# Routing in groups of one head instead of two, with scores made for two queries at a time

## The chip, the core and the metric

The kernel runs on one core of a Trainium2 chip. The metric is the device time of one execution in microseconds. Five engines work side by side, each on its own list of instructions in order, and wait for each other through semaphores: PE (TensorE, matrix products), ACT (ScalarE), DVE (VectorE), POOL (GpSimd) and SP (SyncE, which only issues transfers here).

## The reference, cut to what matters

One layer of an encoder: 512 frames and 16 meta tokens of 1,024 features, a token mixer, then the product-key expert layer (`peer`) that this change is about:

```python
q = jnp.einsum('nd,dhk->nhk', x, w_q)                      # 8 heads, 256 wide
q1, q2 = jnp.split(q, 2, axis=-1)
s1 = jnp.einsum('nhk,hmk->nhm', q1, sub_keys[:, 0])        # 128 keys each
s2 = jnp.einsum('nhk,hmk->nhm', q2, sub_keys[:, 1])
v1, i1 = lax.top_k(s1, PEER_TOPK)                          # PEER_TOPK = 16
v2, i2 = lax.top_k(s2, PEER_TOPK)
cand = (v1[..., :, None] + v2[..., None, :]).reshape(N, PEER_HEADS, 256)
sc, sel = lax.top_k(cand, PEER_TOPK)                       # 16 experts of 16,384
gate = jax.nn.softmax(sc, axis=-1)
a = jnp.einsum('nd,ned->ne', xk, u_emb[ek])                # then gelu(a) * gate
out = jnp.einsum('ne,ned->nd', coef, v_emb[ek])
```

The kernel computes the activations of all 16,384 experts for all frames as 128 "up tiles" and picks with the gates afterwards; so an up tile doesn't need the routing.

## The kernel before, in words

Float32 products are made in three passes: each operand is split into a high half (an ACT copy that rounds, L1438) and a low half (the difference, L1443, by POOL or DVE), and `three_pass` (L368) issues three matmuls for each of 8 slices, 24 in all, for one tile of 128 x 512. Both kinds of tile of this stage are made so: a **query** (`wq`; 16 of them, two for each head, the weights in rings of three) and an **up tile** (`ut`; 24 of the 128 are made in this stage, the others after it).

The stage is `route` (L1483). It begins and ends with a barrier of all engines. Frames are taken in NB = 4 blocks of 128. Queries are taken in groups of G = 4 (two heads); a group gives four **steps** n, one for each block, 16 in all. A step is:

- PE `scores(n)`: a matmul with each of the G queries (L1593) into one bank of PSUM. In its list PE has scores(n+1), then the queries of step n, then the up tiles of step n.
- ACT `copy_scores(n)` to SBUF (L1634). ACT also copies finished queries (`copy_q`, L1628), makes the high half of the query three further on right behind it (`split_q`), and finishes up tiles (gelu, L1474, and the high half of the tile two further on).
- DVE `top16` (L1679) on G key lists of 128: max, match_replace, max, then the indices. `settle` waits after each of the first three groups of instructions for its last one. Then `rank_candidates(n - 1)` does the same on G/2 candidate lists of 256.
- POOL: the low halves of the queries that are three ahead (`low_q`), then the candidate sums of step n (L1822), which wait for DVE's key ranking of step n, then the low halves of the up tiles of step n + 1. All in this order in one list.
- SP: loads of weights, stores of up tiles, and the zeroing of the gate map in 32 stores, dealt over the steps.

Which query and which up tile stands in which step is set by two small tables (L1539, L1540). Behind the steps PE has twelve more up tiles (`sel_up` to 23), beside which DVE turns the ranked places into expert numbers (`hits`, `take`, `sums`, `addresses`) and makes the low halves of these tiles. Behind the stage's barrier, `experts` (L1857) scatters the gates with 384 indirect transfers of POOL, finishes the 104 other up tiles and makes the down products.

The stage before, `mix_rows`, makes queries 0 and 1 at its end. `route` begins with queries 2 and 3, in banks of their own, before the first scores.

Of the kernel before, what the change touches and what calls it, by code (L numbers as in the profile page):

```python
# [23 lines left out]
P = 128  # L24
# [4 lines left out]
NB = FRAMES // P  # L29
# [44 lines left out]
SLOTS = PEER_HEADS * PEER_TOPK  # L74
ZERO_ROWS = 4
WQ_RING = 3
ZERO_STORES = P // ZERO_ROWS


# [1403 lines left out]
def route(c, x_hi, x_lo, places, expert, gates, zeroed, wq, ut, nc, io, sem, sb, psum, ident, iota, gates_d, acts_d, acts_s, **_):  # L1483
# [4 lines left out]

    G = 4
    SETS = 2 * PEER_HEADS
    NG = SETS // G
    STEPS = NG * NB
    K = PEER_TOPK
    sub_keys = sb("sub_keys", [P, SETS, NKEYS], c=c)
    q_t = sb("q_t", [P, 2 * G, FRAMES], c=c)
# [1 line left out]
    work = sb("key_work", [P, G, NKEYS], c=c)  # L1499
    top_v = sb("top_v", [P, NB, SETS, K], c=c)  # L1500
    top_i = sb("top_i", [P, NB, SETS, K], U32, c=c)
    cand = sb("cand", [P, 2, 2, K * K], c=c)
    cand_work = sb("cand_work", [P, 2, K * K], c=c)
    best = sb("best", [P, NB, PEER_HEADS, K], c=c)
    place = sb("place", [P, NB, PEER_HEADS, K], U32, c=c)
    place_half = sb("place_half", [P, 2, PEER_HEADS, K], U32, c=c)
# [29 lines left out]
    sel_up = ROUTE_TILES - SEL * NB  # L1536
    queries, ups, j, t = [], [], G, 0
    for n in range(STEPS):
        q = min(SETS - j, (1, 1, 2, 0)[n % NB])  # L1539
        m = min(sel_up - t, (0, 0, 1, 1)[n % NB] if n + G < SETS else (2, 1, 2, 1)[n % NB])  # L1540
        queries.append(list(range(j, j + q)))
        ups.append(list(range(t, t + m)))
        j, t = j + q, t + m
    assert j == SETS and t == sel_up and STEPS == SETS

    with nc.Block() as block:
        @block.sync
        def _(sp):
            def load_q(j):
                wq.load(sp, io["peer_wq"], j)  # L1550

            def next_up(t):
                ut.load(sp, io["peer_u"], t + ut.RAW)
                ut.store(sp, acts_d, acts_s, t)

            def store_zeros(x):
                rows = slice(x * ZERO_ROWS, (x + 1) * ZERO_ROWS)
                sp.dma_start(gates_d[:, rows], zeros[:].unsqueeze(1).broadcast_to([P, ZERO_ROWS, DENSE])).then_inc(zeroed, 16)

            sp.dma_start(sub_keys[:], io["sub_keys"]).then_inc(keys_in, 16)  # L1560
            sp.wait_ge(zeros_done, 1)
            for t in range(2, ut.RAW):
                ut.load(sp, io["peer_u"], t)
            for j in range(G, G + WQ_RING):
                load_q(j)
            for n in range(STEPS):
                for j in queries[n]:
                    if j + WQ_RING < SETS:
                        load_q(j + WQ_RING)
                for t in ups[n]:  # L1570
                    next_up(t)
                for x in range(n * ZERO_STORES // STEPS, (n + 1) * ZERO_STORES // STEPS):
                    store_zeros(x)
            for t in range(sel_up, ROUTE_TILES):
                next_up(t)

        @block.tensor
        def _(pe):
            def query_bank(j):

                return psum[:, (2 + j if j < G else j % 2), :]

            def query(j):
                wq.product(nc, pe, x_hi, x_lo, j, j % WQ_RING, j < G, query_bank(j))

            def scores(n):
                g, b = divmod(n, NB)
# [10 lines left out]
            def up(t):  # L1598
                ut.product(nc, pe, x_hi, x_lo, t, t % 2, t < 2)

            for j in range(2, G):
                query(j)
            pe.wait_ge(keys_in, 16)
            for n in range(STEPS):
                if n == 0:
# [12 lines left out]
        def _(act):  # L1618
# [3 lines left out]
            def copy_q(j):  # L1622
                g, x = divmod(j, G)
                act.wait_ge(wq.product_done, j + 1)
                if g >= 2:
                    act.wait_ge(s_done, (g - 1) * NB)
                bank = wq.bank[j % 2] if j < 2 or j >= G else psum[:, 2 + j, :]
                nc.scalar.activation(q_t[:, g % 2 * G + x], bank, ACT.Copy).then_inc(wq.bank_read, 1)  # L1628

            def copy_scores(n):  # L1630
                act.wait_ge(s_done, n + 1)
                if n >= 2:
                    act.wait_ge(s_read, n - 1)
                nc.scalar.activation(s[:, n % 2].rearrange("p g m -> p (g m)"), psum[:, 2 + n % 4, :],  # L1634
                                     ACT.Copy).then_inc(s_copied, 1)

            def split_u(t):
# [6 lines left out]

            for j in range(G):
                copy_q(j)
                if j + WQ_RING >= G:
                    split_q(j + WQ_RING)
            for n in range(STEPS):
                if n == 0:  # L1650
                    copy_scores(n)
                if n and n - 1 + G < SETS:
                    for t in ups[n - 1]:
                        finish_up(t)
                if n + 1 < STEPS:
# [5 lines left out]
                if n + G >= SETS:  # L1661
                    for t in ups[n]:
                        finish_up(t)
            act.wait_ge(centered, NB)
# [7 lines left out]
        def _(dve):  # L1672
# [24 lines left out]
            def rank_candidates(n):  # L1697
                g, b = divmod(n, NB)
                dve.wait_ge(cand_done, n + 1)
                top16(2, lambda x: cand[:, n % 2, x], lambda x: cand_work[:, x], lambda x: best[:, b, 2 * g + x],  # L1700
                      lambda x: place[:, b, 2 * g + x], cand_read)

            def low_u(t):
                ut.split_lo(nc.vector, dve, t)
# [98 lines left out]
        def _(pool):  # L1803
# [6 lines left out]
            for j in range(G, G + WQ_RING):  # L1810
                low_q(j)
            for n in range(STEPS):
                g, b = divmod(n, NB)
# [3 lines left out]
                pool.wait_ge(s_read, n + 1)  # L1817
                if n >= 2:
                    pool.wait_ge(cand_read, n - 1)
                for x in range(2):  # L1820
                    head = 2 * g + x
                    last = nc.gpsimd.tensor_tensor(  # L1822
                        cand[:, n % 2, x].rearrange("p (i j) -> p i j", j=K),
                        top_v[:, b, 2 * head].unsqueeze(2).broadcast_to([P, K, K]),
# [383 lines left out]
```

## Time and profile before

| what | us |
|---|---|
| three timed runs | 2107.15, 2117.3, 2119.26 (median 2117.3) |
| the profiled execution: its own time | 2101.18 |
| its span, first to last instruction | 2099.3 |
| in it: up to the routing stage | 422.5 |
| the routing stage | 422.5 to 656.6 |
| gates scattered, up tiles go on | 656.6 to about 1240 |
| remaining up tiles and all down products | to 2099.3 |

The stages were read from the timelines: the first instructions of `route` start at 422.5 (L1558 to L1628), the first up tile of `experts` after the barrier at 657.0. A busy engine is one that has an instruction running; PE's matmuls overlap, so its busy time tells little, and its waits tell more. In a timeline the number in brackets is the time for which the engine sat idle before the instruction, with the instruction or transfer that released it.

### The profile page before, as it was taken

To read this page: it belongs to the slowest core of one execution; us is meant where nothing else is said; L and a number is where in the kernel's file an instruction comes from. 1 tells how busy PE (TensorE), PEld (TensorE's weight loads), DVE (VectorE), ACT (ScalarE), POOL (GpSimd) and SP (SyncE) were. 2 spreads that over 40 slices of the span, in tenths; PEclk is the share of its full clock that TensorE was granted. 3 is DMA by queue.
4 is the path that set the end of the run, shared out by engine and by line. 5 is a ranking of instruction groups with operands and counts; after the bars stand their busy time and mean duration, and the time that the engine had idled before them with its cause. 6 is when DMAs were issued, how large, how long until landed. Compare 5 with 4: busy or idle time off the path is not lost.

```text
span 2099.3 us, 23531 instructions
## 1 busy us (share of the span) xinstructions
PE 1764.5 (84%) x7878; PEld 1430.3 (68%) x7878; DVE 1130.1 (54%) x2971; ACT 576.7 (27%) x924; POOL 909.3 (43%) x800
## 2 busy tenths in 40 slices
PE   5999999999999444663724499999999999999998
PEld 4867778888877233441613278888888888888886
DVE  3269784569986212330503222222236888888886
ACT  4332152332232000110201022222233333333333
POOL 4643200053502667667675640000007767777730
PEclk9999999999999667775856699999999999999999
DMA  4322220258754111220302146444449999999992
GB/s 134 97 61 66 46 70 33 81 197 290 246 196 131 46 38 53 75 76 15 106 16 60 46 127 226 150 141 144 148 141 386 391 376 365 368 374 364 378 357 76
DMA packets 182675, 351.05 MB, mean 167 GB/s; under 512 B 35600, under 2 KB 118928, under 8 KB 182448
## 3 DMA queue, kind: packets, MB, share of 16 engines
q1 hardware_dynamic: 147776, 282.74, 40.4%
q0 software_dynamic: 34816, 67.41, 9.0%
q8 instruction: 27, 0.44, 0.1%
q14 instruction: 56, 0.46, 0.1%
HBM read 289.04 MB, written 61.02 MB: 167 GB/s over the span
## 4 chain that ended last, share of the span: by engine, by line
PE 47%; another core or an unknown queue 14%; issue 5%; ACT 2%; DVE 1%; ACTq 0%; DVEq 0%
PE psum L370 16%; PE psum L372 16%; PE psum L371 16%; ACT ts_hi_u L1438 1%; DVE ts_lo_u L1443 0%; ACT sparse_rows L2068 0%; DVE mixed L1995 0%; DVE mixed L1983 0%; DVE v_lo L1934 0%; ACT v_hi L2051 0%; ACTq L1473 0%; ACT rstd_final L2071 0%; DVE rstd_final L795 0%; DVE rstd_final L799 0%
## 5 line engine op out<-in xcount | busy, mean ns | idle before, releaser
L370 PE MATMUL psum<-x_hi,ts_hi_u 128*128 128x512 f32 x1024 | 419.9, 410 | 188.5 <-issue 108.3
L1443 DVE TENSOR_TENSOR ts_lo_u<-ts_raw_u,ts_hi_u 128x1024 fp32r<-128x1024 f32 x116 | 142.1, 1225 | 681.3 <-ACT ts_hi_u L1438 577.6
L2146 POOL DMA_INDIRECT gate_map<-gate_total,gate_at x384 | 388.5, 1012 | 264.1 <-DVE same_expert L1917 159.8
L372 PE MATMUL psum<-x_hi,ts_lo_u 128*128 128x512 f32 x1024 | 416.3, 407 | 51.6 <-issue 51.5
L371 PE MATMUL psum<-x_lo,ts_hi_u 128*128 128x512 f32 x1024 | 415.2, 406 | 45.6 <-issue 45.5
L370 PEld LDWEIGHTS psum<-x_hi,ts_hi_u 128*128 128x128 f32 x1024 | 202.5, 198 | 250.4 <-issue 148.9
L2134 POOL DMA_INDIRECT sparse_rows<-in_peer_v,v_row x128 | 160.1, 1251 | 425.3 <-PE psum L372 330.9
L1474 ACT ACTIVATE ut_out_u<-psum 128x512 f32<-128x512 f32 x128 | 76.5, 597 | 837.2 <-PE psum L372 395.5
L370 PE MATMUL psum<-v_hi,c_hi 128*128 128x512 f32 x768 | 298.8, 389 | 0.0
L371 PE MATMUL psum<-v_lo,c_hi 128*128 128x512 f32 x768 | 298.8, 389 | 0.0
L372 PE MATMUL psum<-v_hi,c_lo 128*128 128x512 f32 x768 | 298.8, 389 | 0.0
L372 PEld LDWEIGHTS psum<-x_hi,ts_lo_u 128*128 128x128 f32 x1024 | 201.7, 197 | 101.2 <-issue 59.2
L371 PEld LDWEIGHTS psum<-x_lo,ts_hi_u 128*128 128x128 f32 x1024 | 202.5, 198 | 93.1 <-issue 52.9
L2051 ACT ACTIVATE v_hi<-v_raw 128x1024 fp32r<-128x1024 f32 x128 | 135.8, 1061 | 310.0 <-PE psum L372 265.1
L1934 DVE TENSOR_TENSOR v_lo<-v_raw,v_hi 128x1024 fp32r<-128x1024 f32 x128 | 157.0, 1226 | 79.8 <-ACT v_hi L2051 63.4
L2140 POOL DMA_INDIRECT sparse_act<-up_acts_sparse,act_at x128 | 171.8, 1342 | 40.3 <-issue 38.7
L370 PEld LDWEIGHTS psum<-v_hi,c_hi 128*128 128x128 f32 x768 | 144.2, 188 | 30.0
L371 PEld LDWEIGHTS psum<-v_lo,c_hi 128*128 128x128 f32 x768 | 144.2, 188 | 29.8
L372 PEld LDWEIGHTS psum<-v_hi,c_lo 128*128 128x128 f32 x768 | 144.2, 188 | 29.8
L1438 ACT ACTIVATE ts_hi_u<-ts_raw_u 128x1024 fp32r<-128x1024 f32 x128 | 134.5, 1052 | 0.0
L370 PE MATMUL psum<-whi_in,h_hi 128*128 128x512 f32 (+1 forms) x280 | 110.2, 394 | 2.4 <-PEq L268 2.4
L1917 DVE SCALAR_TENSOR_TENSOR same_expert<-expert,gates 128x128 f32<-128x128 f32 x384 | 108.2, 347 | 1.4 <-DVE same_expert L1917 1.4
(235 smaller groups left out, 2345.6 us busy)
## 6 DMA issues: line engine op xcount, KB each, us to landing
ts_raw_u<-in_peer_u SPq DMA_DIRECT2D x128, 512.0 KB
v_raw<-in_peer_v SPq DMA_DIRECT2D x128, 512.0 KB
gate_map<-zeros SPq DMA_DIRECT2D x32, 768.0 KB, 5.9
up_acts<-ut_out_u SPq DMA_DIRECT2D x128, 192.0 KB
act_in<-up_acts SPq DMA_DIRECT2D x128, 192.0 KB
gate_in<-gate_map SPq DMA_DIRECT2D x128, 192.0 KB
raw_in<-in_w_in SPq DMA_DIRECT2D x56, 256.0 KB, 2.8
ts_raw_wq<-in_peer_wq SPq DMA_DIRECT2D x16, 512.0 KB, 7.4
```

Source lines behind the costliest of these rows:

```text
L370: nc.tensor.matmul(out, l_hi, r_hi, start=first, stop=False)
L371: nc.tensor.matmul(out, l_hi, r_lo, start=False, stop=False)
L372: return nc.tensor.matmul(out, l_lo, r_hi, start=False, stop=last)
L1438: nc.scalar.activation(self.hi[:, n % self.slots], self.raw[:, n % self.raws], ACT.Copy).then_inc(self.hi_done, 1)
L1443: eng_ops.tensor_tensor(self.lo[:, n % self.slots], self.raw[:, n % self.raws], self.hi[:, n % self.slots].bitcast(F32), ALU.subtract).the ...
L1474: nc.scalar.activation(self.out[:, i], self.bank[n % 2], ACT.Gelu).then_inc(self.bank_read, 1)
L1917: nc.vector.scalar_tensor_tensor(out=dn.same[:, j % 2], in0=expert[:, b], scalar=expert[:, b, j:j + 1], in1=gates[:, b].rearrange("p h k - ...
L1934: nc.vector.tensor_tensor(dn.v_lo[:, i], dn.v_raw[:, e % RAW], dn.v_hi[:, i].bitcast(F32), ALU.subtract).then_inc(v_lo_done, 1)
L2051: nc.scalar.activation(dn.v_hi[:, i], dn.v_raw[:, e % RAW], ACT.Copy).then_inc(v_hi_done, 1)
L2134: nc.gpsimd.indirect_dma_start(dn.rows[:, r], None, v_rows, bass.IndirectOffsetOnAxis(places["v_row"][:, j:j + 1], 0)).then_inc(row_in[r], 16)
L2140: nc.gpsimd.indirect_dma_start(dn.picked[:, j:j + 1], None, act_cells, bass.IndirectOffsetOnAxis(places["act_at"][:, j:j + 1], 0)).then_in ...
L2146: nc.gpsimd.indirect_dma_start(gate_cells, bass.IndirectOffsetOnAxis(places["gate_at"][:, b, j:j + 1], 0), dn.total[:, b, j:j + 1], None). ...
```

## The change

G becomes 2, one head. A group still has four steps, one for each block, so there are 32 steps in place of 16, each with half the work: two score matmuls in place of four, copied as 128 x 256; two key lists ranked, one candidate list made and ranked. Scores begin once queries 0 and 1 are there; queries 2 and 3 move behind the first scores, and share the two banks of the others. The two tables get new patterns: in a group, steps 0 and 1 have a query each, step 2 an up tile, step 3 nothing; in the last four steps (`n >= ASKING`) there are 2, 1, 1, 1 up tiles. Seven up tiles stand in the first 28 steps and five in the last four, in place of six in the first 12 and six in the last four. Number and size of the tiles, of the transfers and of the ranked lists are the same.

```diff
+EARLY_Q = 4
...
-    G = 4
+    G = 2
+    HEADS = G // 2
     NG = SETS // G
     STEPS = NG * NB
+    ASKING = STEPS - NB
...
     for n in range(STEPS):
-        q = min(SETS - j, (1, 1, 2, 0)[n % NB])
-        m = min(sel_up - t, (0, 0, 1, 1)[n % NB] if n + G < SETS else (2, 1, 2, 1)[n % NB])
+        q = min(SETS - j, (1, 1, 0, 0)[n % NB])
+        m = min(sel_up - t, (0, 0, 1, 0)[n % NB] if n < ASKING else (2, 1, 1, 1)[n % NB])
...
-            for j in range(G, G + WQ_RING):
+            for j in range(EARLY_Q, G + WQ_RING):
                 load_q(j)
...
-            for j in range(2, G):
-                query(j)
             pe.wait_ge(keys_in, 16)
...
-                nc.scalar.activation(s[:, n % 2]..., psum[:, 2 + n % 4, :],
+                nc.scalar.activation(s[:, n % 2]..., psum[:, 2 + n % 4, 0:G * NKEYS],
...
-                if j + WQ_RING >= G:
+                if j + WQ_RING >= EARLY_Q:
                     split_q(j + WQ_RING)
...
-                if n and n - 1 + G < SETS:
+                if n and n - 1 < ASKING:
                     for t in ups[n - 1]:
                         finish_up(t)
...
-                top16(2, lambda x: cand[:, n % 2, x], ...
+                top16(HEADS, lambda x: cand[:, n % 2, x], ...
...
-                for x in range(2):
-                    head = 2 * g + x
+                for x in range(HEADS):
+                    head = HEADS * g + x
```

Two places of the lists show what moves. First POOL, around the low half of the up tile with number 2 (`ts_lo_u`; `ts_lo_wq` is the low half of a query, `cand` the candidate sums). Before, from step 5:

```order
L1443 TENSOR_TENSOR ts_lo_wq<-ts_raw_wq,ts_hi_wq 128x1024
L1822 TENSOR_TENSOR cand<-top_v 128x256 x2
L1443 TENSOR_TENSOR ts_lo_u<-ts_raw_u,ts_hi_u 128x1024
L1443 TENSOR_TENSOR ts_lo_wq<-ts_raw_wq,ts_hi_wq 128x1024 x2
L1822 TENSOR_TENSOR cand<-top_v 128x256 x2
```

And now, from step 8:

```order
L1444 TENSOR_TENSOR ts_lo_wq<-ts_raw_wq,ts_hi_wq 128x1024
L1822 TENSOR_TENSOR cand<-top_v 128x256
L1444 TENSOR_TENSOR ts_lo_wq<-ts_raw_wq,ts_hi_wq 128x1024
L1822 TENSOR_TENSOR cand<-top_v 128x256
L1444 TENSOR_TENSOR ts_lo_u<-ts_raw_u,ts_hi_u 128x1024
L1822 TENSOR_TENSOR cand<-top_v 128x256 x2
```

The low half of the up tile stands in both behind a query's low half and the candidate sums. Before, two more queries follow behind it for the same step, and PE has these two queries ahead of the up tile; now no query of the step follows.

Second ACT at the start of the stage (`q_t` are copied queries, `ts_hi_wq` high halves of query weights, `key_scores` copied scores). Before:

```order
L1628 ACTIVATE q_t<-psum 128x512 x2
L1438 ACTIVATE ts_hi_wq<-ts_raw_wq 128x1024
L1628 ACTIVATE q_t<-psum 128x512
L1438 ACTIVATE ts_hi_wq<-ts_raw_wq 128x1024
L1628 ACTIVATE q_t<-psum 128x512
L1438 ACTIVATE ts_hi_wq<-ts_raw_wq 128x1024
L1634 ACTIVATE key_scores<-psum 128x512 x2
```

And now:

```order
L1628 ACTIVATE q_t<-psum 128x512 x2
L1439 ACTIVATE ts_hi_wq<-ts_raw_wq 128x1024
L1634 ACTIVATE key_scores<-psum 128x256 x2
L1628 ACTIVATE q_t<-psum 128x512
L1439 ACTIVATE ts_hi_wq<-ts_raw_wq 128x1024
L1634 ACTIVATE key_scores<-psum 128x256
```

The first scores are copied two queries earlier, but still behind one high half, that of query 4.

## Rows read from the trace of the kernel before

**Rows 1.** Windows by stage: busy us of each engine, PE clock, DMA share, GB/s.

```profile
422.50:656.60 234.10, 224.25 (x1040) 186.91 (x1040) 198.03 (x853) 71.14 (x99) 76.24 (x57) 0.99 0.65 224
656.60:1240.00 583.40, 305.43 (x1057) 225.91 (x1057) 158.60 (x812) 67.45 (x88) 388.51 (x384) 0.70 0.21 59
```

**Rows 2.** Timeline of ACT, routing: start, us, instruction, idle before and releaser.

```profile
566.99 0.60 ACT L1474 ACTIVATE ut_out_u<-psum 128x512 f32<-128x512 f32 x1 [4.32 <-PE psum L372]
...
573.34 0.60 ACT L1474 ACTIVATE ut_out_u<-psum 128x512 f32<-128x512 f32 x1 [4.31 <-PE psum L372]
...
578.78 0.60 ACT L1474 ACTIVATE ut_out_u<-psum 128x512 f32<-128x512 f32 x1 [3.89 <-PE psum L372]
...
654.79 0.60 ACT L1474 ACTIVATE ut_out_u<-psum 128x512 f32<-128x512 f32 x1 [3.89 <-PE psum L372]
```

**Rows 3.** Waits of PE in the routing stage: us, times, longest.

```profile
PE psum L370 <- DVE ts_lo_u L1443: 4.7, 2, 3.2
...
PE psum L1593 <- ACT q_t L1628: 2.0, 1, 2.0
PE psum L370 <- POOL ts_lo_u L1443: 1.3, 1, 1.3
```

**Rows 4.** Timeline of DVE, the first ranking of four lists.

```profile
438.30 0.87 DVE L1683 MAX8 top_v<-key_scores 128x8 f32<-128x128 f32 x4 [14.68 <-ACT key_scores L1634]
439.21 0.09 DVE L1686 MATCH_VALUE_LOAD key_work<-top_v,key_scores 128x8 f32 x1
...
443.41 0.85 DVE L1683 MAX8 top_v<-key_scores 128x8 f32<-128x128 f32 x4
```

**Rows 5.** Timeline of DVE, the first ranking of two candidate lists.

```profile
450.06 0.76 DVE L1683 MAX8 best<-cand 128x8 f32<-128x256 f32 x2 [1.49 <-POOL cand L1822]
...
454.15 0.85 DVE L1683 MAX8 top_v<-key_scores 128x8 f32<-128x128 f32 x4
```

**Rows 6.** One line's instructions: count, ns min/median/max.

```profile
L1683 DVE MAX8 top_v<-key_scores x64: 271/276/295, 438.3 to 577.6; 128x8 f32<-128x128 f32 x64
```

**Rows 7.** Timeline of DVE at the end of the ranking.

```profile
587.29 0.75 DVE L1683 MAX8 best<-cand 128x8 f32<-128x256 f32 x2
...
591.38 1.20 DVE L1443 TENSOR_TENSOR ts_lo_u<-ts_raw_u,ts_hi_u 128x1024 fp32r<-128x1024 f32 x1
```

**Rows 8.** The key table's load, from issue to landing.

```profile
DMA to landing us min/median/max: 4.9/4.9/4.9
```

**Rows 9.** Timeline of ACT at the routing stage's start.

```profile
432.55 1.06 ACT L1438 ACTIVATE ts_hi_wq<-ts_raw_wq 128x1024 fp32r<-128x1024 f32 x1 [8.91 <-DMA ts_raw_wq<-in_peer_wq]
...
437.68 0.60 ACT L1634 ACTIVATE key_scores<-psum 128x512 f32<-128x512 f32 x1 [1.21 <-PE psum L1593]
```

**Rows 10.** Timeline of ACT, a query copied, the next one's high half.

```profile
487.46 0.60 ACT L1628 ACTIVATE q_t<-psum 128x512 f32<-128x512 f32 x1 [0.78 <-PE psum L372]
490.67 1.06 ACT L1438 ACTIVATE ts_hi_wq<-ts_raw_wq 128x1024 fp32r<-128x1024 f32 x1 [2.62 <-DMA ts_raw_wq<-in_peer_wq]
```

**Rows 11.** Timeline of POOL behind that high half.

```profile
491.81 2.41 POOL L1443 TENSOR_TENSOR ts_lo_wq<-ts_raw_wq,ts_hi_wq 128x1024 fp32r<-128x1024 f32 x1 [2.00 <-ACT ts_hi_wq L1438]
494.18 1.20 POOL L1822 TENSOR_TENSOR cand<-top_v 128x256 f32<-128x256 f32 x2
495.34 2.42 POOL L1443 TENSOR_TENSOR ts_lo_u<-ts_raw_u,ts_hi_u 128x1024 fp32r<-128x1024 f32 x1
```

**Rows 12.** Timeline of PE, a tile after a pause (weight loads left out).

```profile
690.63 0.79 PE L370 MATMUL psum<-x_hi,ts_hi_u 128*128 128x512 f32 x1 [4.51 <-DVE ts_lo_u L1443]
...
694.63 0.63 PE L370 MATMUL psum<-x_hi,ts_hi_u 128*128 128x512 f32 x1
...
695.58 0.40 PE L370 MATMUL psum<-x_hi,ts_hi_u 128*128 128x512 f32 x1
```

**Rows 13.** Windows after a pause of PE: columns as Rows 1.

```profile
436.00:438.00 2.00, 2.00 (x11) 2.00 (x11) 0.00 (x0) 0.79 (x2) 2.00 (x2) 0.50 0.55 33
588.00:590.00 2.00, 2.00 (x10) 1.67 (x9) 1.90 (x9) 0.00 (x0) 0.00 (x0) 1.00 1.06 397
```

More of the change, by code:

```diff
@@ L1501, in route @@
     top_i = sb("top_i", [P, NB, SETS, K], U32, c=c)
-    cand = sb("cand", [P, 2, 2, K * K], c=c)
-    cand_work = sb("cand_work", [P, 2, K * K], c=c)
+    cand = sb("cand", [P, 2, HEADS, K * K], c=c)
+    cand_work = sb("cand_work", [P, HEADS, K * K], c=c)
     best = sb("best", [P, NB, PEER_HEADS, K], c=c)
@@ L1543, in route @@
         j, t = j + q, t + m
-    assert j == SETS and t == sel_up and STEPS == SETS
+    assert j == SETS and t == sel_up
     with nc.Block() as block:
@@ L1579, in query_bank @@
             def query_bank(j):
-                return psum[:, (2 + j if j < G else j % 2), :]
+                return wq.bank[j % 2]
             def query(j):
-                wq.product(nc, pe, x_hi, x_lo, j, j % WQ_RING, j < G, query_bank(j))
+                wq.product(nc, pe, x_hi, x_lo, j, j % WQ_RING, j < 2, query_bank(j))
             def scores(n):
@@ L1626, in copy_q @@
                     act.wait_ge(s_done, (g - 1) * NB)
-                bank = wq.bank[j % 2] if j < 2 or j >= G else psum[:, 2 + j, :]
-                nc.scalar.activation(q_t[:, g % 2 * G + x], bank, ACT.Copy).then_inc(wq.bank_read, 1)
+                nc.scalar.activation(q_t[:, g % 2 * G + x], wq.bank[j % 2], ACT.Copy).then_inc(wq.bank_read, 1)
             def copy_scores(n):
@@ L1633, in copy_scores @@
                     act.wait_ge(s_read, n - 1)
-                nc.scalar.activation(s[:, n % 2].rearrange("p g m -> p (g m)"), psum[:, 2 + n % 4, :],
+                nc.scalar.activation(s[:, n % 2].rearrange("p g m -> p (g m)"), psum[:, 2 + n % 4, 0:G * NKEYS],
                                      ACT.Copy).then_inc(s_copied, 1)
@@ L1660, in _ @@
                         split_q(j + WQ_RING)
-                if n + G >= SETS:
+                if n >= ASKING:
                     for t in ups[n]:
@@ L1699, in rank_candidates @@
                 dve.wait_ge(cand_done, n + 1)
-                top16(2, lambda x: cand[:, n % 2, x], lambda x: cand_work[:, x], lambda x: best[:, b, 2 * g + x],
-                      lambda x: place[:, b, 2 * g + x], cand_read)
+                top16(HEADS, lambda x: cand[:, n % 2, x], lambda x: cand_work[:, x], lambda x: best[:, b, HEADS * g + x],
+                      lambda x: place[:, b, HEADS * g + x], cand_read)
             def low_u(t):
@@ L1809, in _ @@
                 ut.split_lo(nc.gpsimd, pool, t)
-            for j in range(G, G + WQ_RING):
+            for j in range(EARLY_Q, G + WQ_RING):
                 low_q(j)
```

## The prediction

> **What bounds the kernel now.** I read four views, in this order. The windows by stage come first [rows 1]: the change lies in the stage from 422.5 to 656.6 us. In it PE has matmuls running for 224 of 234 us at a granted clock of 0.99, DVE is busy for 198, and ACT and POOL for about 75 each, so only PE or DVE can set this stage's end. In the next stage PE is busy for 305 of 583 us and POOL for 389. That stage begins behind a barrier of all engines and depends on nothing that the change touches but its start, so every us by which routing ends later is, to first order, a us of the whole.
>
> Then ACT's timeline, because ACT takes up each finished tile and so marks PE's pace [rows 2]. Two tiles with nothing between are 578.78 - 573.34 = 5.44 us apart. A tile with one score step ahead of it takes 573.34 - 566.99 = 6.35, so a score step of four queries costs PE 0.91. The last tile is done at 654.8, and the barrier follows at 656.6: PE ends the stage.
>
> Then PE's waits [rows 3]: 4.7 + 2.0 + 1.3 = 8.0 us. PE's work is 38 tiles x 5.44 = 206.7, and 16 score steps x 0.91 = 14.6. With the waits that is 229.3 of the 232.3 between 422.5 and 654.8. PE has next to nothing to give, and it depends on the order of the others' lists.
>
> Last DVE's timeline. Ranking four lists takes 443.41 - 438.30 = 5.11 us [rows 4], ranking two candidate lists 454.15 - 450.06 = 4.09 [rows 5]. Sixteen of both make 147 us of the 153 between 438.3, where ranking begins, and 591.4, where it ends [rows 4, 7]. So PE and DVE are nearly balanced through the steps.
>
> **The change part by part.**
>
> *Split ranking, DVE.* The same 64 + 32 lists are ranked, but the three waits of each ranking come twice as often. One MAX8 lasts 0.276 us [rows 6], four in a row 0.87 [rows 4], so starts are (0.87 - 0.276) / 3 = 0.20 apart and 0.08 of each is covered by the next. Behind a wait that cover is lost, and 439.21 - (438.30 + 0.87) = 0.04 comes on top [rows 4]. That is 0.12 for a wait; six new ones for each old step make 0.72, over 16 steps 11.5 us. A new step takes (5.11 + 4.09 + 0.72) / 2 = 4.96 us, and 32 of them 159 us. The Trainium skill weighs against this sum: "VectorE: DVE Perf Modes", section "The DRAIN you can't avoid", says that a semaphore behind every operation costs nothing over one behind the last. By it the 11.5 would be 0. The rows show the overlap that a wait takes away, and I go by them; no wait of the forecast's sum hangs on it.
>
> *Start.* Scores no longer stand behind queries 2 and 3, but behind the key table. It lands 4.9 us after its issue [rows 8], at 427.4, so PE waits 4.9 where it waited 2.0 [rows 3]: +3 on PE. DVE gains less than the 10.9 us of two tiles: ACT's copy of the first scores still has the high half of query 4 ahead, whose weights land at 432.5 [rows 9]. Ranking starts at about 433.7 in place of 438.3.
>
> *The up tile behind its low half.* This is the term that decides. In steps 8 to 11, 12 to 15 and 16 to 19 the order on PE is: scores, query, scores, query, scores, up tile. This tile's low half is POOL's, and in POOL's list it stands behind the low half that follows the second of these queries. That low half waits for ACT's high half, which reuses the query's slot and so waits for PE to finish this very query. The trace has the same chain once at full length: the query's copy starts at 487.46, the high half at 490.67 behind its load [rows 10], then POOL makes a low half, the sums of two heads, and the up tile's low half until 497.76 [rows 11]. That is 10.3 us. Before, it lay beside two further queries, 10.9 us of PE's work, and PE waited 1.3 [rows 3]. Now there is one score step of 0.45 beside it. The chain itself is shorter by one head's sums, 0.6. With the load's wait as in the row it is 9.7, without any (2.7 less) 7.0; I take 8.4, the middle, since the load is issued at the same point of the cycle but behind one zeroing store less. So PE waits 8.4 - 0.5 = 7.9, and a group takes 3 x 5.44 + 4 x 0.45 + 7.9 = 26.0 us where DVE's work is 4 x 4.96 = 19.9. Three groups: 23.7 - 1.3 = +22.4; the ends are 6.5 and 9.2 for each, or +18 and +26.
>
> *The later groups.* In steps 20 to 23 only the first query still has a successor, so a part of the chain lies beside the second query: 8.4 less 5.9 of query and scores would leave 2.5, but the candidate sums of step 21 wait for DVE, which is a step late by then; I take 5, between 2.5 and 7.9. In steps 24 to 31 there are six up tiles whose low halves stand behind sums paced by DVE's 4.96 us for a step: I take 2 + 3.5, between 0 and 10 in all. Sum +10.5.
>
> *The end.* The waits before tiles 12 and 14, 4.7 us [rows 3], came about because PE was ready before DVE had ranked. PE is now the later one, so they go: -4.7, or 0 at worst.
>
> *The clock.* Behind a pause of 4.5 us [rows 12] matmuls start (694.63 - 690.63) / 9 = 0.44 us apart, where a tile at full rate has 5.44 / 24 = 0.23; from 695.58 they are fast again. So the first 4 to 5 us after such a pause run at the lower level, 1.2 in place of 2.4 GHz, and cost 10 x 0.21 = 2 us. A pause of 2.0 did so too (at 436), one of 3.2 did not (at 588) [rows 3, 13]. Four pauses of 5 to 8 us make +8, between 0 (DVE could hide them) and +14. The start had a slow stretch before and has one now: 0.
>
> *At nothing.* ACT's 16 added copies are halves of the old ones; ACT is idle for two thirds of the stage [rows 1]. POOL's sums are as many as before. On SP every load and store keeps its place against its tile; zeroing goes from two stores a step to one, and must be done only before the scatters. If that cover went, a store in front of a load would lengthen the chain above, which its upper end holds.
>
> **Sum:** 3 + 22.4 + 10.5 - 4.7 + 8 = +39. DVE's catching up inside the blocked groups overlaps a little of the clock's term; I take off 2. Routing ends at 654.8 + 37 = 692 and the profiled execution goes from 2101.2 to 2138. That execution is faster than all three timed runs. The middle of the four times (2101.2, 2107.2, 2117.3, 2119.3) is 2112; the forecast for a median is 2112 + 37 = **2149 us**.
>
> **Rivals.**
>
> *DVE's pace (not slower).* If the up tiles' low halves come in time, PE waits 5 at the start and then runs through 26 tiles and all scores until 427.4 + 141.4 + 14.6 = 583.4, while DVE ranks until 433.7 + 158.7 = 592.4 instead of 591.4. The tail behind the ranking is as before, so routing ends 1 us later: 2113. For it: the balance is good on paper, 18.1 us of PE's work to 19.9 of DVE's in a group. Against it: the chain is forced by three lists in order. It decides if PE's waits for `ts_lo_u` stay below 2 us a group. By the page of the Trainium skill named above, the 11.5 us of waits would be nothing as well, PE would end the stage 6 us earlier (583.4 + 12 x 5.44 = 648.7), and the time would be about 2106.
>
> *The clock stays low.* If after each of the four pauses a whole tile and more runs at the lower level, each costs 5.4 in place of 2.0: +14, or 2163. For it: in the next stage, where PE is busy for half of the time, the mean clock is 0.70 [rows 1]. Against it: there the pauses are far longer.
>
> *The next stage gives it back, or more.* Its POOL work is 384 scatters, and PE's tiles wait for loads there. A shift of its start could shuffle these by some 10 us in either direction (the runs' own spread is 12). A gain of over 1% would need 60 us of it.
>
> **Chances.** The chain as forecast: 0.78. DVE's pace: 0.13. The clock stays low: 0.07. A gain out of the next stage: 0.02. About 1%, 21 us, is what a measurement of this kernel tells from no change. The chain at its lowest (3 + 18 + 2.5 - 4.7 + 0 = +19) lies just below it. So slower by over 1%: 0.82; within 1%: 0.16; faster: 0.02. The range takes in the chain's lower bound on the fastest timed run (2107 + 19) and the low clock on the slowest (2119 + 37 + 14): about 2127 to 2172.
>
> **What would show it.** PE's waits in the stage: `ts_lo_u` of POOL, five to seven times, 30 us or more in total, the longest 7 to 9; PE waits 5 us for the key table; the tiles after the pauses at half rate, the stage's clock near 0.9; first key ranking at 433 to 435; last candidate ranking at 615 to 625; a step of DVE without waits 4.96. The barrier comes at 685 to 700. I am wrong if PE's waits for `ts_lo_u` stay below 10 us, or if the next stages don't keep their 1443 us within 15.

## The result and the profile after

The changed kernel takes a median of 2139.6 us over four runs (2127.02 to 2142.17) beside 2116.37 for the kernel before (2107.15 to 2119.26), a ratio of 1.0148 with a 95% interval of 1.009 to 1.0205. Ratios in this document are made from the runs within 1.5% of the fastest of the same kernel and are not the quotients of the two medians, which is 1.011 here (23.2 us). Its profiled execution took 2138.91 us with a span of 2137.1, against 2101.18 and 2099.3. Routing's last up tile is done at 689.03 instead of 654.79: +34.2 us. The span is longer by 37.8.

The windows by stage of the changed kernel, columns as in [rows 1]:

```profile
422.50:600.00 177.50, 143.21 (x645) 119.11 (x646) 138.08 (x696) 42.01 (x73) 66.50 (x50) 0.90 0.58 206
600.00:700.00 100.00, 97.77 (x436) 80.78 (x435) 72.60 (x161) 31.85 (x44) 9.01 (x6) 1.00 0.54 170
700.00:1270.00 570.00, 287.82 (x984) 211.83 (x983) 154.61 (x809) 62.95 (x82) 387.55 (x384) 0.70 0.20 58
```

The loss is all in the first window: PE is idle for 34 of 177.5 us and its granted clock is 0.90. What PE waited for between 418 and 700 us (total, times, longest), to be laid beside [rows 3]:

```profile
PE psum L371 <- POOL ts_lo_u L1444: 29.8, 5, 7.3
PE psum L1596 <- DMA sub_keys<-in_sub_keys: 5.6, 1, 5.6
```

The waits of before for DVE's `ts_lo_u` (4.7) and for `q_t` (2.0) are gone, as is POOL's 1.3. The timeline of PE has each pause in brackets, with what ended it:

```profile
426.90 2.08 PE L1596 MATMUL psum<-sub_keys,q_t 128*128 128x128 f32 x8 [5.61 <-DMA sub_keys<-in_sub_keys]
...
484.68 0.79 PE L371 MATMUL psum<-x_hi,ts_hi_u 128*128 128x512 f32 x1 [7.06 <-POOL ts_lo_u L1444]
...
511.99 0.80 PE L371 MATMUL psum<-x_hi,ts_hi_u 128*128 128x512 f32 x1 [7.33 <-POOL ts_lo_u L1444]
...
538.98 0.80 PE L371 MATMUL psum<-x_hi,ts_hi_u 128*128 128x512 f32 x1 [7.00 <-POOL ts_lo_u L1444]
...
564.23 0.80 PE L371 MATMUL psum<-x_hi,ts_hi_u 128*128 128x512 f32 x1 [5.11 <-POOL ts_lo_u L1444]
...
595.30 0.50 PE L371 MATMUL psum<-x_hi,ts_hi_u 128*128 128x512 f32 x1 [3.27 <-POOL ts_lo_u L1444]
```

The first three pauses come 27 us apart, once in each group of four steps, the fourth 25 us later and the last behind the queries. One of them, followed back on ACT and then on POOL:

```profile
498.36 0.60 ACT L1628 ACTIVATE q_t<-psum 128x512 f32<-128x512 f32 x1 [4.25 <-PE psum L373]
502.36 1.06 ACT L1439 ACTIVATE ts_hi_wq<-ts_raw_wq 128x1024 fp32r<-128x1024 f32 x1 [3.40 <-DMA ts_raw_wq<-in_peer_wq]
503.32 0.36 ACT L1634 ACTIVATE key_scores<-psum 128x256 f32<-128x256 f32 x1
504.26 0.60 ACT L1628 ACTIVATE q_t<-psum 128x512 f32<-128x512 f32 x1 [0.57 <-PE psum L373]
505.58 1.06 ACT L1439 ACTIVATE ts_hi_wq<-ts_raw_wq 128x1024 fp32r<-128x1024 f32 x1 [0.72 <-DMA ts_raw_wq<-in_peer_wq]
```

```profile
503.49 2.36 POOL L1444 TENSOR_TENSOR ts_lo_wq<-ts_raw_wq,ts_hi_wq 128x1024 fp32r<-128x1024 f32 x1 [12.39 <-ACT ts_hi_wq L1439]
505.81 0.62 POOL L1822 TENSOR_TENSOR cand<-top_v 128x256 f32<-128x256 f32 x1
506.71 2.34 POOL L1444 TENSOR_TENSOR ts_lo_wq<-ts_raw_wq,ts_hi_wq 128x1024 fp32r<-128x1024 f32 x1 [0.28 <-ACT ts_hi_wq L1439]
509.01 0.62 POOL L1822 TENSOR_TENSOR cand<-top_v 128x256 f32<-128x256 f32 x1
509.59 2.35 POOL L1444 TENSOR_TENSOR ts_lo_u<-ts_raw_u,ts_hi_u 128x1024 fp32r<-128x1024 f32 x1
```

From the second query's copy (504.26) to the end of the up tile's low half (511.94) it is 7.7 us, and the tile starts at 511.99. This is the chain of [rows 10, 11] (10.3 us there), with nothing but a score step of PE's beside it. POOL had been idle for 12.39 us just before: it is late by its order, not by its load.

DVE without waits, the candidate rankings of three steps in a row:

```profile
587.19 0.41 DVE L1683 MAX8 best<-cand 128x8 f32<-128x256 f32 x1
...
592.15 0.41 DVE L1683 MAX8 best<-cand 128x8 f32<-128x256 f32 x1
...
597.12 0.41 DVE L1683 MAX8 best<-cand 128x8 f32<-128x256 f32 x1
```

A step is 4.97 us. Ranking begins at 432.50, and DVE goes on to the gates at 626.47, where before did so at 592.50.

### The profile page after: what moved, and what is told of

It reads as the page before. It is cut to its first block, busy times and chain, and to the rows that moved or that the text cites. A ratio compares the mean times of both kernels' runs of the same rounds, so it can differ in the third digit from the quotient of the medians.

```text
span 2137.1 us, 23589 instructions
## 1 busy us (share of the span) xinstructions
PE 1771.1 (83%) x7878; PEld 1434.6 (67%) x7878; DVE 1140.7 (53%) x2971; ACT 578.1 (27%) x940; POOL 914.0 (43%) x800
## 4 chain that ended last, share of the span: by engine, by line
PE 44%; another core or an unknown queue 16%; issue 3%; ACT 2%; DVE 2%; ACTq 0%; DVEq 0%
PE psum L373 15%; PE psum L371 15%; PE psum L372 15%; ACT ts_hi_u L1439 1%; DVE ts_lo_u L1444 1%; DVE same_expert L1917 0%; ACT sparse_rows L2068 0%; DVE mixed L1995 0%; DVE mixed L1983 0%; DVE v_lo L1934 0%; ACT ut_out_u L1475 0%; ACT v_hi L2051 0%; ACTq L1474 0%; ACT rstd_final L2071 0%
## 5 line engine op out<-in xcount | busy, mean ns | idle before, releaser
L2140 POOL DMA_INDIRECT sparse_act<-up_acts_sparse,act_at x128 | 174.0, 1359 | 40.1 <-issue 40.1
L373 PEld LDWEIGHTS psum<-v_hi,c_lo 128*128 128x128 f32 x768 | 144.1, 188 | 29.9
L372 PEld LDWEIGHTS psum<-v_lo,c_hi 128*128 128x128 f32 x768 | 144.1, 188 | 29.9
```

The lines of the kernel that those rows point to most:

```text
L372: nc.tensor.matmul(out, l_hi, r_lo, start=False, stop=False)
L373: return nc.tensor.matmul(out, l_lo, r_hi, start=False, stop=last)
L2140: nc.gpsimd.indirect_dma_start(dn.picked[:, j:j + 1], None, act_cells, bass.IndirectOffsetOnAxis(places["act_at"][:, j:j + 1], 0)).then_in ...
```

## The experiments

The sets of runs fell on different chips. In three sets the kernel before takes 2105 to 2123 us, in the fourth 1758.75 (see the last section). Routing lies ahead of the stage in which they differ, so its traces compare across chips; medians are compared only with those of the same set. The place from which routing starts differs between traces by up to 2.8 us: PE's first scores start at 426.90 in the first trace of the changed kernel and at 429.65 in the last. Some of the expectations call the kernel with the low half a whole group earlier e6, and the one with the first scores first as well e7.

### The changed kernel again

> The changed kernel once more, beside the others of this call. Theory (the up tile's low half behind the query's chain in POOL's list): routing's last tile at 687 to 692 us in the profile, PE waits for ts_lo_u 28 to 32 us in all, and the time 1.1 to 1.8% over the kernel before. Rival (later stages give part of the shift back): the same profile of the routing stage, but a ratio below 1.011.

Beside before at 2123.37 us it took 2157.96, ratio 1.018 (1.014 to 1.0221). Waits for POOL's `ts_lo_u`: 28.1 us in 6, longest 6.9; last routing tile 689.35. All this is as the theory had it. A third time, in a later set:

> The changed kernel once more, beside e6 and the combined kernel, for a reading of all of them against one set of runs of before. Theory A (the +34 us of the last routing tile are passed on one to one, whatever the clock of the stages behind is): the median is 32 to 36 us above before's; if before runs at about 1759 us again, where no stage behind had a granted clock of 0.7, that is a ratio of 1.018 to 1.021, against 1.015 and 1.018 where before took 2116 and 2123 us. Theory B (the stages behind stretch or absorb part of the shift by their clock): a difference outside 28 to 40 us.

It took 2145.22 us beside 2105.14, ratio 1.0244 (1.0176 to 1.0311), with waits of 29.4 in 5 and the last tile at 694.07, 2.8 of it from the later start. The difference of medians, 40.1 us, lies just beyond what theory A and even 28 to 40 allowed, but the 17 runs of before in that set spread from 2080.64 to 2117.59, so it doesn't tell the theories apart. The three intervals have 1.0176 to 1.0205 in common.

### The low half one step earlier

```diff
             for n in range(STEPS):
...
+                if n + 1 < ASKING:
+                    for t in ups[n + 1]:
+                        if t >= 2:
+                            ut.split_lo(nc.gpsimd, pool, t)
                 for j in queries[n]:
...
-                for t in ups[n + 1] if n + 1 < STEPS else []:
+                for t in ups[n + 1] if ASKING <= n + 1 < STEPS else []:
```

> The changed kernel, with one thing moved on POOL: the low half of the next step's up tile comes ahead of the query's low half and the candidate sums, in all steps but the last four. Theory: PE's four waits of 5 to 7 us before tiles 2 to 5 go below 1 us each and with them the slow clock behind them; routing's last tile falls from 689 to 656 to 662, since DVE's 32 steps of 4.96 us then set the pace, and the time comes within 0.4% of the kernel before. Rival A (DVE's split ranking is the real limit, and PE's waits only mirror it): the waits change places but the last tile stays above 675. Rival B (loads or ACT): PE's waits move to ts_hi or to the queries, last tile 665 to 680.

It took 2145.15 us, ratio 1.0121 (1.008 to 1.0163): better than the changed kernel of the same set by 12.8 us, but the waits only shrank from 28.1 to 19.6 us in 5. The last tile came at 679.67, 9.7 earlier, of which 0.8 is an earlier start (PE's first scores at 427.11 and 427.96). The size that the theory gave was wrong, and the last tile is above the 675 of rival A, though the waits didn't change places. POOL's timeline says why:

```profile
500.39 2.37 POOL L1444 TENSOR_TENSOR ts_lo_wq<-ts_raw_wq,ts_hi_wq 128x1024 fp32r<-128x1024 f32 x1 [8.20 <-ACT ts_hi_wq L1439]
502.71 0.62 POOL L1826 TENSOR_TENSOR cand<-top_v 128x256 f32<-128x256 f32 x1
503.29 2.34 POOL L1444 TENSOR_TENSOR ts_lo_u<-ts_raw_u,ts_hi_u 128x1024 fp32r<-128x1024 f32 x1
```

The up tile's low half had only passed the second of the group's two query low halves. The first was still ahead of it, and with it ACT's high half, for which POOL waited 8.20 us. So this run doesn't decide on rival A; the next one does.

### The low half a whole group earlier

The edit is shown against the kernel just above:

```diff
-                if n + 1 < ASKING:
-                    for t in ups[n + 1]:
+                if n % NB == NB - 1 and n + 3 < ASKING:
+                    for t in ups[n + 3]:
```

> The changed kernel, with POOL making the low half of an up tile a whole group of four steps earlier (just ahead of the candidates of the step before a group begins), so that it stands behind none of the low halves of query weights that came ahead of it. In the kernel with the low half only a step earlier TensorE still waited 3.9 to 4.3 us four times, because ACT's high half of the query weight and its DMA wait stood between. Theory A (the order on POOL's queue is the whole cost): TensorE's waits for this low half are under 1 us in groups 2 to 6, four falls of the clock go too, and the last routing tile ends at 656 to 664 us (before 654.8, changed kernel 689.0 and 689.4); ratio 1.000 to 1.006. Theory B (the ranking on DVE with its 96 more waits, or the query weights' loads, is a second bound close below): the waits for the low half vanish but others for q_t or ts_lo_wq take their place, last tile 665 to 678, ratio 1.007 to 1.012.

On the chip where before takes 1758.75 us it took 1774.1, ratio 1.0086 (1.0072 to 1.01). The ratio and the last tile (671.09) lie in the ranges of theory B, but not for its reason: the five pauses are gone, and no other wait took their place in the groups; there is one new wait, once, at the first tile behind the queries. PE's timeline, and POOL's with the low half that ends it:

```profile
558.15 1.13 PE L1596 MATMUL psum<-sub_keys,q_t 128*128 128x128 f32 x8 [0.76 <-ACT q_t L1628]
574.99 0.80 PE L371 MATMUL psum<-x_hi,ts_hi_u 128*128 128x512 f32 x1 [15.71 <-POOL ts_lo_u L1444]
```

```profile
572.02 0.62 POOL L1826 TENSOR_TENSOR cand<-top_v 128x256 f32<-128x256 f32 x1 [4.35 <-DVE top_i L1694]
572.60 4.68 POOL L1444 TENSOR_TENSOR ts_lo_u<-ts_raw_u,ts_hi_u 128x1024 fp32r<-128x1024 f32 x2
```

PE has run ahead until it has nothing left: the next tile's low half stands behind the candidate sums of step 27, which DVE paces. DVE now goes on to the gates at 608.54, and the last tile is 17.9 us earlier than in the changed kernel and 16.3 later than before. The run again, beside the changed kernel on one of the slower chips:

> The kernel with the low half a whole group earlier once more, beside the changed kernel. It took 15.4 us more than before (1774.1 against 1758.75), its last routing tile ended 16.3 us later. Theory A: it lies 17 to 20 us under the changed kernel here, which is what the order on POOL's queue and the falls of the clock behind it cost. Theory B: less than 12 us under it; then much of the difference to the earlier readings came from the chip and not from the order.

2123.71 us against 2145.22, 21.5 us less, with the same 15.7-us wait; the last tile came at 669.48, and from PE's first scores on that is 22.9 us less than in the changed kernel (241.49 and 264.42). Theory A had the cause, and its 17 to 20 us are a little too few. Beside before the ratio is 1.0153 (1.0099 to 1.0207).

### And the first scores first

```diff
             for j in range(G):
                 copy_q(j)
-                if j + WQ_RING >= EARLY_Q:
-                    split_q(j + WQ_RING)
...
                 if n + 1 < STEPS:
                     copy_scores(n + 1)
+                if n == 0:
+                    split_q(EARLY_Q)
```

> The kernel with the low half a whole group earlier, and ACT copies the first scores ahead of the high half of the fifth query weight, in place of behind it (that copy stood behind a DMA wait of 8.1 us and ended at 432.5 in the changed kernel). Theory A (DVE's ranking is what is late once TensorE's pauses are gone): the first ranking starts at 428 to 429, the whole routing moves with it by 3 to 4 us, last tile 653 to 660, ratio 0.998 to 1.004. Theory B (TensorE's own work sets the pace then): ranking starts earlier, but the last tile stays within 1 us of the kernel without this edit.

1773.92 us, ratio 1.0085 (1.0071 to 1.0098), the same as without this edit. Ranking starts at 429.02, 4.0 us earlier, and then waits for the first candidates, whose sums stand on POOL behind the low half of another query:

```profile
440.76 0.43 DVE L1683 MAX8 best<-cand 128x8 f32<-128x256 f32 x1 [6.17 <-POOL cand L1826]
```

Where the kernel without it waited 2.82 there. So 3.35 of the 4.0 are given back, and the last tile comes at 669.97, 1.1 earlier. Theory A had the start right and the gain wrong; theory B had the gain nearly (within 1 us), but not for its reason: PE still waits 15.71 us for the same low half.

### And both remaining waits

```diff
-        m = min(sel_up - t, (0, 0, 1, 0)[n % NB] if n < ASKING else (2, 1, 1, 1)[n % NB])
+        m = min(sel_up - t, (0, 0, 1 + (n == ASKING - 2), 0)[n % NB] if n < ASKING else 1)
...
-                for j in queries[n]:
+                for j in queries[n] if n >= 2 else []:
...
                 last.then_inc(cand_done, 1)
+                for j in queries[n] if n < 2 else []:
+                    low_q(j + WQ_RING)
```

> On top of e7: the seventh and eighth up tile are both asked of TensorE at step 26 (in e6 and e7 it stood 15.7 us before the eighth, whose low half POOL makes behind the candidates of step 27, while the weights of that tile had lain there since 543 us), and in steps 0 and 1 POOL makes the low half of the query weight behind the candidates and not ahead of them (DVE waited 6.2 us for the first candidates in e7). Theory A (what is left of the loss is TensorE without work while DVE ranks, and DVE's pace of 4.97 us a step against 9.15 for two): the wait for ts_lo_u falls from 15.7 to under 9 us, ranking ends at 595 to 600 (e7 607.4, before 592.5), the last routing tile ends at 658 to 664, ratio 1.001 to 1.005. Theory B (the wait only moves to the next tile, since its high half stands behind a score copy on ACT that waits for DVE): waits for ts_lo_u stay above 12 us in all, last tile 665 to 670, ratio 1.006 to 1.009.

```profile
577.30 0.79 PE L371 MATMUL psum<-x_hi,ts_hi_u 128*128 128x512 f32 x1 [11.47 <-POOL ts_lo_u L1444]
```

One tile more runs ahead of the wait, which becomes 11.5 us; the last tile comes at 667.87. The wait lies between the theories, the last tile in the range of theory B. The reason that theory B gave doesn't hold for this tile: ACT had made its high half by 567.65, and POOL made the low half 7 us later, behind the candidate sums for which it waited for DVE:

```profile
566.59 1.06 ACT L1439 ACTIVATE ts_hi_u<-ts_raw_u 128x1024 fp32r<-128x1024 f32 x1
```

```profile
574.33 0.62 POOL L1826 TENSOR_TENSOR cand<-top_v 128x256 f32<-128x256 f32 x1 [4.35 <-DVE top_i L1694]
574.90 2.35 POOL L1444 TENSOR_TENSOR ts_lo_u<-ts_raw_u,ts_hi_u 128x1024 fp32r<-128x1024 f32 x1
```

DVE goes on to the gates at 605.32, later than the 595 to 600 of theory A. The median is 2121.18 us beside 2105.14 for before and 2123.71 for e6 in the same set; one of its twelve runs took 2068.93 and the others 2107.68 to 2134.88, so the medians say little. In the trace the last tile is 13 us behind before, 1.9 of it from a later start of routing. No version built on the change beat the kernel before.

### Work in the pauses

```diff
+    FILL = {2: 28, 3: 28, 4: 28, 5: 20}
...
                 for t in ups[n]:
+                    if t in FILL:
+                        pe.wait_ge(ut.bank_read, t - 1)
+                    for m in range(FILL.get(t, 0)):
+                        nc.tensor.matmul(ut.bank[t % 2], x_hi[:, m % KT, 0:P], x_hi[:, m % KT], start=True, stop=True)
                     up(t)
```

> The changed kernel, with 28, 28, 28 and 20 matmuls of no use on TensorE ahead of up tiles 2 to 5, where it waited 7.1, 7.3, 7.0 and 5.1 us (each is 0.2 us or so; they write a bank that the tile's first product then starts afresh). It leaves the waits and takes only the fall of the clock behind them. Theory A (each fall costs 2 us of tile behind it, as the prediction had it): first matmuls of tiles 2 to 5 are 0.50 us and not 0.80, the last routing tile ends 6 to 9 us earlier than 689, ratio 1.010 to 1.014. Theory B (the fall costs next to nothing, since the next wait for the low half is shorter by what the tile took longer): the last tile stays within 2 us of 689, and the waits left grow by what the tiles gain; ratio 1.015 to 1.018.

Ratio 1.0168 (1.0154 to 1.0182), 1787.21 us beside 1758.75. Tiles 2 to 5 find the clock up, but a pause of 3.30 us at 588.24 now has a fall behind it that the first trace of the changed kernel did not have. The last tile comes at 684.73, and from the first scores at 427.50 that is 257.2 us against 262.1: 4.9 less, for four falls taken away and one added. The last tile lies between the theories. The ratio lies in the range of theory B, but the changed kernel has no run on this chip to set beside it.

### The ranking split, and nothing else

The kernel before with its rankings made in halves:

```diff
-                top16(G, lambda x: s[:, n % 2, x], lambda x: work[:, x], lambda x: top_v[:, b, g * G + x],
-                      lambda x: top_i[:, b, g * G + x], s_read)
+                for y in range(0, G, 2):
+                    top16(2, lambda x: s[:, n % 2, y + x], lambda x: work[:, y + x], lambda x: top_v[:, b, g * G + y + x],
+                          lambda x: top_i[:, b, g * G + y + x], s_read if y else None)
```

(the candidates' one likewise, with 1 and 1).

> The kernel before, with groups of two heads as they were, but each ranking on DVE done in two halves, as in the change: key lists two and two, candidate lists one and one. Steps, tiles and all other lists are as before. Theory (a wait behind a shorter row costs 0.12 us, 96 new ones): ranking ends 11 to 12 us later than 591.4 us, routing's last tile at 664 to 667, time +0.4 to +0.6%. By the Trainium skill's page on VectorE (a semaphore costs nothing extra): ranking ends at 591 and nothing moves.

> The kernel before with its rankings made in halves (2 and 2 lists, 1 and 1 candidates: the 96 more waits of the change and nothing else of it), once more where a run of before varies by 2 us and not by 28. In its first trace a group of four took 9.94 us on DVE against 9.15 in before, 16 x 0.79 = 12.6 us more work, yet the last routing tile came only 6.1 us later, since 5.2 us of waits for candidates went. Theory A (DVE's pace is bound together with those waits): the median is 5 to 8 us above before's, ratio 1.003 to 1.0045. Theory B (the whole 12.6 us show): ratio 1.006 to 1.008. Theory C (the trace was a mishap and waits cost nothing): under 1.001.

The second set of runs was meant for the chip on which before varies by 2 us, but fell on one where it varies by 37. Ratios 1.0034 (1.0006 to 1.0061) and 1.0112 (1.0049 to 1.0175); last routing tile at 660.86 and 664.00. Ranking ended at 597.5 in the first trace, 6 us later than before and not the 11 to 12 of the first theory. A group of four lists takes 9.94 us on DVE against 9.15, so 16 of them cost 12.6 us. From the first ranking to the gates it is 161.4 and 162.1 us against 154.2: +7.2 and +7.9, which is the 12.6 less the 5.2 us that DVE waited for candidates before and no longer does (0 and 0.6). Theory C is out, and so is the first text's rival that nothing moves. The interval of the second set lies above the range of A and takes in that of B; the first set's ratio and both traces (+7.2 and +7.9 us up to the gates, not +12.6) speak for A. The choice between them stays open as far as the medians go.

### A late barrier, and nothing else

The kernel before with 14 idle comparisons on DVE at the end of routing (each 2.3 us):

```diff
+            for _ in range(14):
+                settle(nc.vector.tensor_tensor(
+                    hit[:].rearrange("p t h k (j i) -> p (t h k) j i", i=2),
...
+                    ALU.is_equal))
```

> The kernel before, with 14 comparisons of 2.25 us that nobody reads appended to DVE's list at the end of routing, so that the barrier comes 31 us later and nothing else of the stage changes. Theory (a later barrier is a longer run, one to one): time +29 to +35 us, +1.4 to +1.65%, and 1443 us from barrier to end within 8. Rival (the next stage gives part of a shift back): +15 to +25 us.

```profile
PE psum L370 <- PEq L1546: 32.4, 1, 32.4
```

PE waits 32.4 us at the barrier, 30.1 more than the 2.3 of the kernel before. The median went from 2123.37 to 2153.31, +29.9, ratio 1.0153 (1.0113 to 1.0194, or 24 to 41 us). So the medians pass on what routing loses one to one, within that interval. The part of the theory on the trace missed: from the barrier to the end it is 1458.7 us (2144.5 - 685.8) where the trace of before has 1442.3, 16 more and not within 8. That trace of before is of another set and of its fastest execution, 2101.18 us where the median of before here is 2123.37.

## Why the prediction was right

Forecast: last tile +37 us, a profiled execution of 2138 and a median of 2149. Measured: +34.2, 2138.91, and 2139.6 (2145.22 and 2157.96 in the other sets). As differences: +37.7 between the two profiled executions, +23.2 between the medians of the first set, +34.6 and +40.1 between those of the others.

| step of the prediction | forecast | measured |
|---|---|---|
| start: PE's waits | +3 | +3.6 (5.6 for 2.0) |
| three groups | +22.4 | +20.1 (7.06 + 7.33 + 7.00 - 1.3) |
| later groups | +10.5 | +8.4 (5.11 + 3.27) |
| waits at the end | -4.7 | -4.7 |
| clock, less overlap | +6 (8 - 2) | +6.8, as the rest of +34.2; the four falls alone 7.5 |

**The chain.** A pause was forecast at 7.9 us, from a chain of 8.4 between bounds of 7.0 and 9.7; the traces have 6.7 to 7.6. The chain itself is 7.7 and the load's wait in it 0.72, where I had put the middle between 0 and 2.7. A group takes 27.3 us (511.99 - 484.68) and not 26.0. The sum had booked the clock apart: 18.1 us of tiles and scores and 7.3 of a pause leave 1.9 for the fall.

That the order on POOL's queue causes the pauses is shown, not only argued: with the same work in another order they shrink to 3.4 to 4.3 us and then vanish, and the last tile comes 9.7 and 17.9 us earlier. The 17.9 are about half of the +34.2; beside the changed kernel of its own set, from the first scores on, it was 22.9. No run took away the rest.

**The rival of DVE's pace** said that with the low halves in time routing would end 1 us later than before. That was too good by 15 us, for two reasons that the later experiments show. It counted 26 tiles ahead of the end of ranking as work that PE could do at any time, but those behind step 27 are tied to DVE's ranking through the candidate sums ahead of them on POOL, which waited 4.35 us for DVE in the row at 572.02; PE stood 15.7 us without work. And it left DVE no waits at all, where in the trace with the pauses gone 7.1 us for scores and 3.7 for candidates remained. The mechanism to which it pointed exists; it is the next bound and not one that equals the old time. How much of the 16.3 us is DVE's longer step and how much the place of the tiles in the two tables is not shown: one more tile ahead of the wait shortened it by 4.2 us, and no run of the new order had the old ranking.

**Split ranking.** Forecast 4.96 us a step, measured 4.97. In the kernel before with split rankings 96 more waits cost 12.6 us of DVE's time, 0.13 each. The reading of it is that of the prediction: short operations in a row overlap (four MAX8 of 0.276 us in 0.87), and a wait parts them. The Trainium skill, "VectorE: DVE Perf Modes", section "The DRAIN you can't avoid", says of eight copies that a semaphore behind every one costs nothing over one behind the last. For the operations of the ranking the measurement shows otherwise. In the changed kernel DVE waits for others for 31 us between its first ranking and the gates, so its longer steps are not what PE waits for in the groups; with the pauses taken out those waits are 13 us, and DVE's pace comes through.

**The clock.** What a fall costs can be read from the time between an up tile's first matmul and the start of ACT's gelu on it. At the tile of 595.30, without a fall, it is 5.77 us; at the four with one it is 7.33, 7.34, 7.48 and 8.40. Two of the ends:

```profile
492.01 0.60 ACT L1475 ACTIVATE ut_out_u<-psum 128x512 f32<-128x512 f32 x1 [11.07 <-PE psum L373]
...
601.07 0.60 ACT L1475 ACTIVATE ut_out_u<-psum 128x512 f32<-128x512 f32 x1 [7.81 <-PE psum L373]
```

So a fall costs 1.6 to 2.6 us and the four 7.5, for a forecast of 2 each. In the kernel with work in the pauses the first ones take 5.77 and the one at 588.24, with the added fall, 8.53: 7.5 less 2.8 is 4.7, and 4.9 were gained. The shape that I took as their sign, a first matmul of 0.8 us, is not a safe one: in the kernel with the low half one step earlier the first matmul behind a pause of 3.41 us is 0.50, and the clock is down a moment later. Its windows (columns as in [rows 1]):

```profile
481.60:484.00 2.40, 2.33 (x7) 1.84 (x8) 2.30 (x10) 0.38 (x1) 2.40 (x3) 0.66 0.52 137
484.00:486.50 2.50, 2.50 (x9) 1.99 (x8) 2.40 (x16) 0.00 (x0) 0.54 (x1) 0.65 0.20 82
486.50:489.00 2.50, 2.50 (x14) 2.05 (x13) 2.40 (x11) 0.00 (x0) 0.62 (x1) 1.00 0.00 0
```

So that kernel kept its falls (its five tiles take 7.36 to 7.39 us), and its 9.7 us are the 8.5 us of waits that it lost, the 0.8 of its earlier start and little else. The rival in which the clock stays low for a whole tile is out. In the changed kernel, around the tile at 484.68, it is up again some 3 us behind the tile's start (0.50, then 0.80, then 1.00):

```profile
484.60:487.00 2.40, 2.32 (x6) 1.84 (x7) 2.30 (x13) 0.00 (x0) 0.64 (x2) 0.50 0.54 125
487.00:489.50 2.50, 2.50 (x10) 2.04 (x9) 2.40 (x13) 0.00 (x0) 0.00 (x0) 0.80 0.22 90
489.50:492.00 2.50, 2.50 (x13) 2.06 (x12) 2.40 (x13) 0.00 (x0) 0.62 (x1) 1.00 0.00 0
```

**The later stages** kept their time: from the last routing tile to the end it is 1448.1 us (2137.1 - 689.03), against 1444.5, and from the barrier on 1445.9 against 1442.3. In the changed kernel's other two traces it is 1460.2 and 1453.8 from the barrier on, so the first of these is beyond the 15 us within which the prediction had said it would stay; in its set before takes 22 us more than in the trace of before. The late barrier, compared within one set, gave +29.9 us for 30.1. Within the 1448.1 us the last scatter comes 567.6 us behind the last routing tile instead of 580.3, and what follows takes 880.5 instead of 864.2; this exchange stays unexplained.

**The start.** Ranking began at 432.50 for a forecast of 433.7, and the last candidate ranking ended at 623.4, within the 615 to 625 given. PE's waits for POOL's `ts_lo_u` were 29.8 us in all where 30 or more were forecast. Two roundings of the prediction are off without effect: 4 x 4.96 is 19.8, and 2119 + 37 + 14 is 2170.

**The median** came 9.4 us under the forecast for one. The term that was mis-sized is the last, the 11 us from a profiled execution to the median. For before they fit: its profiled execution (2101.18) is the fastest of its five, and its median in this set is 2116.37. The changed kernel's own profiled execution (2138.91) lies in the middle of its four, so there they were nothing. So +37 is borne out by the traces (37.8) and by the medians of the other sets, and not by the medians of this one, which are 23.2 us apart; no trace explains the difference, and before alone spreads over 12 us in this set and 37 in another.

## What to carry to other kernels

When the work ahead of a tile on the matmul engine is made shorter, look at the tile's own supplier: on the queue that makes its operand, count what stands ahead and how late that may start, since an in-order queue that is idle for nearly two thirds of the time (POOL, busy for 66.5 of 177.5 us) can still hold up the busiest engine by 7 us a group. Moving the late operation ahead of one neighbour only shows the next; and once it is out of the way, the rival bound must be worked out with its own ties and not as free work, which here hid 15 us. Splitting each ranking into halves cost DVE 0.13 us for each added wait, with no work added.

## What the runs showed of the hardware

- The same kernel before takes 1758.75 us on one chip (nine runs within 2.3 us) and 2105 to 2123 in the sets on others. Up to the barrier behind routing the traces of one kernel agree: the last routing tile of the kernel with the low half a group earlier ends at 671.09 on the one and at 669.48 on the other (that of the changed kernel at 689.03, 689.35 and 694.07 on the slower ones). The difference is the stage with the scatters. The kernel with the low half a group earlier, from the chip on which it took 1774 us and from one on which it took 2124, columns as in [rows 1]:

```profile
700.00:1000.00 300.00, 300.00 (x1325) 248.43 (x1324) 162.19 (x751) 85.05 (x110) 232.64 (x222) 1.00 0.53 159
1000.00:1270.00 270.00, 270.00 (x1192) 223.56 (x1192) 76.61 (x76) 83.89 (x110) 182.15 (x173) 1.00 0.53 165
```

```profile
700.00:1270.00 570.00, 290.04 (x980) 213.08 (x981) 147.68 (x750) 64.49 (x84) 370.25 (x370) 0.70 0.20 58
```

  On the one PE never pauses in that stage and 159 GB/s flow beside the scatters; on the other they are 58. In the changed kernel's trace, from such a chip, ACT waits there to write an activated tile, up to 61.5 us at a time, for something that the profile names only as remote:

```profile
ACT ut_out_u L1475 <- remote: 374.6, 18, 61.5
```

  The granted clock of 0.70 goes with PE's pauses in that stage: where it has none, it is 1.00. Why they come on the one chip and not on the other was not tried and stays open.
- A pause of PE of 3.27 us, ahead of the same tile in three traces of the changed kernel, had a fall of the clock behind it in two (0.50 from 597.5 to 602.5 in the last) and none in one (1.00 from 595.0 on). The length of a pause alone does not tell whether the clock falls.
